# A different choice of seven-product tiles, and a different order in the first tiles, of four gated feed-forwards

## The reference, cut to what matters

```python
def rms_norm(x, w):
    xf = x.astype(jnp.float32)
    y = xf * lax.rsqrt(jnp.mean(xf * xf, axis=-1, keepdims=True) + EPS)
    return (y * w.astype(jnp.float32)).astype(x.dtype)

def swiglu(h, w_gate, w_up, w_down):
    return (jax.nn.silu(h @ w_gate) * (h @ w_up)) @ w_down

    for i in range(DEPTH):
        x = x + 0.5 * swiglu(rms_norm(x, ffn1_norm[i]), ffn1_w_gate[i], ffn1_w_up[i], ffn1_w_down[i])
        x = x + hybrid_mixer(...)
        x = x + 0.5 * swiglu(rms_norm(x, ffn2_norm[i]), ffn2_w_gate[i], ffn2_w_up[i], ffn2_w_down[i])
```

## Time and profile before

| | us |
|---|---|
| median of three runs | 2572.62 (2571.46 to 2574.76) |
| the profiled execution | 2572.15 |
| its span | 2570.4 |
| TensorE busy (matmuls) | 2488.7, 97% |
| VectorE, ScalarE, GpSimd busy | 1424.2, 1182.5, 1231.6 |
| mean granted TensorE clock | 0.991 of full speed |
| w_hi of a unit on ScalarE, mean | 1.01 |
| w_lo of a unit on GpSimd, mean | 2.36 |
| t_lo on GpSimd, one of two, mean | 2.60 |
| a unit's load, issue to landing, median | 3.5 |

### The profile page before, as it was taken

How to read it: one execution, slowest core, us unless ns; L and a number is a source line. 1 busy time by engine, 2 the same in 40 slices (tenths; PEclk the granted TensorE clock), 3 DMA queues, 4 the chain that set the end, 5 groups by cost and what they waited for, 6 DMA issues and landing times.

```text
span 2570.4 us, 34829 instructions
## 1 busy us (share of the span) xinstructions
PE 2488.7 (97%) x14086; PEld 2080.9 (81%) x14086; DVE 1424.2 (55%) x2049; ACT 1182.5 (46%) x1737; POOL 1231.6 (48%) x610
## 2 busy tenths in 40 slices
PE   8999999999989999999999989999999998999999
PEld 6888888777778898777878778898877766898887
DVE  6344352878563443586766753453587466443345
ACT  5332243568443333567455542332555675332333
POOL 3654654222455555446544255555444124555544
PEclk9999999999999999999999999999999999999999
DMA  3322333111313323222110123333332112323323
GB/s 130 115 95 87 115 111 111 58 58 50 106 60 109 103 91 107 82 89 84 50 34 27 53 96 92 106 99 95 96 98 82 41 50 75 114 91 99 107 91 123
DMA packets 61774, 223.43 MB, mean 87 GB/s; under 512 B 6704, under 2 KB 6832, under 8 KB 61488
## 3 DMA queue, kind: packets, MB, share of 16 engines
q1 hardware_dynamic: 60928, 218.07, 27.2%
q10 hardware_dynamic: 688, 3.15, 0.3%
HBM read 219.10 MB, written 2.10 MB: 86 GB/s over the span
## 4 chain that ended last, share of the span: by engine, by line
PE 75%; DVE 13%; ACT 6%; issue 3%; POOL 2%; DMA 1%; SPq 0%; DVEq 0%; ACTq 0%
PE ps L426 6%; PE ps L425 6%; PE ps L424 6%; PE ps L582 5%; PE ps L583 5%; PE ps L584 5%; PE ps L531 3%; PE ps L532 3%; PE ps L533 3%; PE ps L523 2%; PE ps L522 2%; PE ps L521 2%; PE ps L887 2%; PE ps L888 2%; PE ps L889 2%
## 5 line engine op out<-in xcount | busy, mean ns | idle before, releaser
L2859 POOL TENSOR_TENSOR w_lo<-raw,w_hi 128x1024 fp32r<-128x1024 f32 (+1 forms) x405 | 952.5, 2359 | 1199.0 <-ACT w_hi L445 1198.6
L445 ACT ACTIVATE w_hi<-raw 128x1024 fp32r<-128x1024 f32 (+1 forms) x405 | 409.6, 1012 | 479.6 <-PE ps L426 282.1
L582 PE MATMUL ps<-x_hi,w_hi 128*128 128x512 f32 x784 | 309.3, 395 | 13.1 <-DVE x_lo L483 7.4
L583 PE MATMUL ps<-x_lo,w_hi 128*128 128x512 f32 x784 | 306.5, 391 | 0.0
L584 PE MATMUL ps<-x_hi,w_lo 128*128 128x512 f32 x784 | 306.1, 390 | 0.0
L424 PE MATMUL ps<-mid_hi,w_hi 128*128 128x512 f32 x736 | 286.3, 389 | 0.0
L425 PE MATMUL ps<-mid_lo,w_hi 128*128 128x512 f32 x736 | 286.3, 389 | 0.0
L426 PE MATMUL ps<-mid_hi,w_lo 128*128 128x512 f32 x736 | 286.3, 389 | 0.0
L793 DVE SCALAR_TENSOR_TENSOR h<-ps,h 128x512 f32<-128x512 f32 x128 | 87.5, 691 | 266.8 <-PE ps L426 266.8
L636 ACT ACTIVATE ff_gate<-ff_gate 128x512 f32<-128x512 f32 x88 | 55.4, 630 | 372.3 <-DVE ff_gate L752 321.2
L2866 POOL TENSOR_TENSOR t_lo<-t_sum,t_hi 128x1024 fp32r<-128x1024 f32 x78 | 201.2, 2601 | 8.9 <-ACT t_hi L450 8.9
(11 more groups left out here) (449 smaller groups left out, 5780.0 us busy)
## 6 DMA issues: line engine op xcount, KB each, us to landing
raw<-in_units_dram SPq DMA_DIRECT2D x406, 512.0 KB, 3.5
...
```

What stands on the lines that cost most here:

```text
L445: nc.scalar.activation(w_hi[:, n % W_SLOTS, begin:], raw[:, n % RAW_SLOTS, begin:], ACT.Copy).then_inc(s_whi, 1)
L582: nc.tensor.matmul(out, hi, x_hi[:, k, :], start=(k == 0), stop=False)
L583: nc.tensor.matmul(out, hi, x_lo[:, k, :], start=False, stop=False)
L2859: nc.gpsimd.tensor_tensor(w_lo[:, n % W_SLOTS, begin:], raw[:, n % RAW_SLOTS, begin:], w_hi[:, n % W_SLOTS, begin:].bitcast(F32), ALU.subt ...
```

## The change

- **STRASSEN.** In chunks 1 and 2 of every feed-forward the seven-product tiles are 0, 1, 3, 5 instead of 0, 2, 4; in chunk 3 (four tiles) 0, 1, 3 instead of 0, 2. In chunk 0 of FF2 to FF4 they are 3 and 5 instead of 2 and 4; chunk 0 of FF1 keeps tile 4. The total is 51 instead of 39, and 37 plain tiles are left of 49.
- **Banks and buffers by parity.** A seven-product tile uses the banks and the ff_gate and ff_up halves of its own parity (pair = t % 2), as plain tiles do; the lent bank is 2 + pair of the other group. x_part lies elsewhere in SBUF.
- **The sequence of two neighbours.** If tile t + 1 is by seven products too, strassen_first(t + 1) is called inside strassen_rest(t), ahead of mid_lo of t. The weight sums of a chunk's tile 1 are made after side 1's additions to h of the chunk before.
- **Chunk 0.** ScalarE does rstd before the w_hi of units 3 and 4 (FF2 to FF4), or after them and before x_part (FF1), and each sx_hi comes behind a tile's mid_hi; VectorE makes both sx_lo after the tile two before the first seven-product one. FF1's activation sums are made behind its tiles 0 and 1. TensorE waits for the sums ahead of the second product of the first such tile, not ahead of the first.

```diff
-STRASSEN = (((4,), (0, 2, 4), (0, 2, 4), (0, 2)),) + (((2, 4), (0, 2, 4), (0, 2, 4), (0, 2)),) * 3
+STRASSEN = (((4,), (0, 1, 3, 5), (0, 1, 3, 5), (0, 1, 3)),) + (((3, 5), (0, 1, 3, 5), (0, 1, 3, 5), (0, 1, 3)),) * 3
...
-        x_part = place("x_part", M, [P, 8, HT])
+        x_part = place("x_part", M + 24 * KB, [P, 8, HT])
...
-            a, b, c = ps[:, 4 * g, 0:HT], ps[:, 4 * g + 1, 0:HT], ps[:, 4 * (g ^ 1) + 3, 0:HT]
+            a, b, c = ps[:, 4 * g + 2 * pair, 0:HT], ps[:, 4 * g + 2 * pair + 1, 0:HT], ps[:, 4 * (g ^ 1) + 2 + pair, 0:HT]
...
             pe.wait_ge(s_free, need + 1)
+            if first:
+                pe.wait_ge(s_xsum, 15 * w.ffn + 15)
             sum_product(b, 1, summed(1), True)
...
-            act_x_parts(act, w, own)
+            if not late:
+                act_x_parts(act, w, own)
...
                 if half == 0:
-                    ahead = 3
-                    act_ahead(act, n0, 0, 0)
-                    act_x_sums(act, w)
-                    act_ahead(act, n0, 0, 1)
+                    ahead = 2
                     if late:
-                        act_ahead(act, n0, 0, 2)
+                        act_ahead(act, n0, 0, 0)
+                        act_ahead(act, n0, 0, 1)
                         act_rstd(act, w, 4 * (g ^ 1), eps)
+                        act_x_parts(act, w, own)
                     else:
                         act_rstd(act, w, 4 * (g ^ 1), eps)
-                        act_ahead(act, n0, 0, 2)
+                        act_ahead(act, n0, 0, 0)
+                        act_ahead(act, n0, 0, 1)
...
                     nc.scalar.activation(mid_hi[:, t, :], product, ACT.Copy).then_inc(s_mhi, 1)
+                    if half == 0 and picked[0] - 3 <= t < picked[0] - 1:
+                        act_x_sum(act, w, t - picked[0] + 3)
...
-                    nc.vector.tensor_tensor(up, up, ff_gate[:, 0, :], ALU.mult).then_inc(s_prod, 1)
+                    nc.vector.tensor_tensor(up, up, ff_gate[:, pair, :], ALU.mult).then_inc(s_prod, 1)
+                    if t + 1 in picked:
+                        strassen_first(t + 1)
                     dve.wait_ge(s_mhi, mids + t + 1)
...
                     if t in picked:
-                        strassen_first(t)
+                        if t - 1 not in picked:
+                            strassen_first(t)
...
+                        if half == 0 and late and t < 2:
+                            dve_x_sums(dve, w, own, t)
+                        if half == 0 and t == picked[0] - 2:
+                            dve_x_sums_lo(dve, w, 0)
+                            dve_x_sums_lo(dve, w, 1)
...
                     dve_add_to_h(dve, w, tiles // 2, side, scale, gain, half == 3)
-                    if side == 0 and half < 3:
-                        dve_weight_sums(dve, S_OF[n0 + 3 * tiles])
+                    if half < 3 and side in STRASSEN[w.ffn][half + 1]:
+                        dve_weight_sums(dve, S_OF[n0 + 3 * tiles + 2 * side])
```

More of the change, by code:

```diff
@@ new lines, in dve_x_sums_lo, with dve_ffn @@
+        def dve_x_sums_lo(dve, w, i):
+            dve.wait_ge(s_xpart, 10 * w.ffn + 8 + i + 1)
+            nc.vector.tensor_tensor(sx_lo[:, 2 * i:2 * i + 2, :, :].rearrange("p a b t -> p (a b t)"),
+                                    sx_sum[:, 2 * i:2 * i + 2, :, :].rearrange("p a b t -> p (a b t)"),
+                                    sx_hi[i][:, :, :, :].rearrange("p a b t -> p (a b t)").bitcast(F32), ALU.subtract).then_inc(s_xsum, 1)
+        def dve_ffn(dve, w, scale, own, gain, split_p=False, late=False):
+            if not late:
+                dve_x_sums(dve, w, own, 0)
+                dve_x_sums(dve, w, own, 1)
@@ L714, in plain @@
                         dve_weight_sums(dve, S_OF[n0 + 2 * picked[0]])
-                    if half == 0 and t == 0:
-                        dve_x_sums_lo(dve, w)
                     dve.wait_ge(s_used, n0 + u + 2)
@@ L751, in strassen_rest @@
                     dve.wait_ge(s_sv, 7 * x + 5)
-                    nc.vector.tensor_tensor(ff_gate[:, 0, :], gate, rstd[:, :], ALU.mult).then_inc(s_free, 1)
+                    nc.vector.tensor_tensor(ff_gate[:, pair, :], gate, rstd[:, :], ALU.mult).then_inc(s_free, 1)
                     dve.wait_ge(s_used, n + 2)
```

65 lines of the change are left out of this document (29 added, 36 removed).

## The result

The kernel after takes 2657.59 us (median of four runs, 2652.22 to 2661.06) against 2572.43 (2571.46 to 2574.76) for the kernel before on the same chip: ratio 1.0324, 95% interval 1.0312 to 1.0336. The medians differ by 85.2 us.

The account below looks back on a forecast made before the run. The prediction took the kernel to be as long as TensorE's matmul stream and its gaps (busy 2488.7 of 2570.4 us). Seven terms summed to +73.7 on 2572.15, giving 2645.9 us, range 2608 to 2676.

Parts of the forecast that it names:

- forecast case: Whole kernel: stall at chunk ends, stall at heads, clock falling at most ends; 2645.9 us, chance 0.55.
- d: Tile 5 in 8 chunks of six tiles: TensorE waits some 0.6 us for t_lo; +4.8 us, bounds 0 and 12.
- f: Chunk 0 of FF1: the 5.70 us gap goes, but t_lo for tile 4 comes late; +4.5 us, bounds -8 and +8.
- g: Behind the chunk-end stops: TensorE's clock falls to half at most of 15, 1.5 us each; +22.5 us, bounds 0 and 51.
- a: Three more seven-product tiles in each feed-forward, 12 in all, each 0.84 us shorter than plain; -10.1 us.
- b: End of 15 chunks, ahead of the squares: TensorE waits 3.65 us for the last tile's second eviction; +54.8 us.
- c: Head of 12 chunks: GpSimd's turn between VectorE's weight-sum subtractions makes TensorE wait 1.3 us; +15.6 us.
- e: Chunk 0 of FF2 to FF4: lost time falls from 13.8 to 7.7 us each; -18.4 us, bounds -40 and 0.
- Full clock: Rival at chunk ends: the stops come but the clock does not fall; 2623 us, chance 0.20.
- long falls: Rival at chunk ends: each gap brings 6.8 us at half rate, 3.4 lost; 2674 us, chance 0.13.
- The end wait is met in time: Rival at chunk ends: banks_free is already there, so no stop or clock fall; 2568.5 us, chance 0.06.
- First tiles give back all: Rival in chunk 0 of FF2 to FF4: no gap left, -40 us there; 2624 us, chance 0.06 shared with another case.

Follow-up runs that it names:

- x_end: The kernel after, with TensorE starting the last squares in the three free banks and waiting only ahead of the lent fourth bank: 2578.19 us, ratio 1.0015.
- x_head: The kernel after, with VectorE's weight sums of tile 1 moved behind tile 0's copy and add: 2641.52 us, ratio 1.0267.
- x_d: The kernel after, with ScalarE's w_hi copy for the unit four further on taken ahead of a seven-product tile's own Silu: 2658.03 us, ratio 1.0328.
- x_ff1: The kernel after, with FF1's first chunk alone back in the old order: 2655.2 us, ratio 1.0316.
- x_c0: The kernel after, with chunk 0 of FF2 to FF4 reordered: both sx_hi right behind the norm, sx_lo behind tile 0's evictions: 2658.38 us, ratio 1.0323.
- x_dummy: The kernel after, end wait kept, with 15 unread matmuls of 512 columns ahead of it: 2633.51 us, ratio 1.0233.

## Why the prediction was right, point by point

It gave 2646 us, range 2608 to 2676, and slower with a chance of 0.94; 2657.6 came. The forecast case held (end stall, head stall, the clock falls), and the sum was 73.7 where 88.9 were measured between the profiled executions and 85.2 between the medians. What is missing lies in d, f and g, all three too small. Differences of whole chunks give the terms:

| term | predicted | measured | |
|---|---|---|---|
| a, 12 more seven-product tiles | -10.1 | -10.1 | rates as before |
| b, 15 stops at the end | +54.8 | +54.8 | 14 of 3.63, one of 3.98 |
| c, 12 heads | +15.6 | +14.6 | 1.22 each |
| d, tile 5's weights | +4.8 | +11.9 | the rest of chunks 1 to 3, net of 2.5 lost there before |
| e, chunk 0 of FF2 to FF4 | -18.4 | -18.4 | -6.4, -6.1, -5.9 without their ends |
| f, chunk 0 of FF1 | +4.5 | +7.8 | 87.84 against 80.03 for its tiles |
| g, the clock behind the stops | +22.5 | +28.0 | 1.87 on average |
| sum | +73.7 | +88.6 | |

- **b** was right in place, cause and size. The chain that had run beside a plain tile is 3.75 us from the last matmul's start. x_end shows that it is a matter of one bank: three were free all the time.
- **c** was right: GpSimd got one turn inside the four subtractions. The Trainium skill (SBUF - State Buffer, section "SBUF: two separate sides") has the lock held for one instruction; 1.78 us for the one subtraction beside GpSimd's half unit and 0.68 or 0.69 for the others agree. x_head gave back 14.7.
- **g** was mis-sized, by counting on ends without a fall and by taking the price from the middle. In the profiled execution all 15 stops were followed by half clock, thirteen at 1.6 to 1.8 us and two at 2.7 and 3.0, where the half clock lasted 6.8 us. The window 9 to 20 of the earlier trace rows, where single gaps of 1.7 us left the clock at 1.00, was no guide for 3.6. In x_head and x_d it was 15 of 15 again, in x_ff1 14 and in x_c0 13, so it is not quite certain each time. The Trainium skill (TensorE: Matmul & The Clock Gate, section "HAM oscillation - how this bites in real kernels") says that a wait in a loop, if it is long enough, puts the array back to half rate each time round; the 15 falls here agree, and the 14 and 13 of the two other executions are short of "each time".
- **d** was the term most off, and came out at its upper bound of 12; 9.4 us of it are at tile 5. The 11.6 us from the unit's arrival to t_lo held: from the start of the sums to that of t_lo it is 889.19 to 898.17, 8.98 us, and in the earlier trace rows 9.00. The step that was off is the one ahead of it, the moment at which unit 11's slot comes free. The prediction had GpSimd split unit 9 by T0 + 40.0, at 2.4 us a unit. Units 8 and 9 took 2.85 each, beside VectorE's product and mid_lo, and the split ended at 885.54, T0 + 41.1. So unit 11 landed at T0 + 44.7 instead of 43.7, and TensorE went on at T0 + 56.2 instead of 55.3. It asked at T0 + 55.2 instead of 54.7, since tile 3 had lost some 0.4 already. That makes 1.0 us in this chunk and 0.9 to 2.0 in the eight, where 0.6 was forecast. The losses at tile 3, up to 0.65 us, had been put at nothing.
- **e** had its wait right even in time: TensorE was to stand from 740.5 to 745.4; moved by FF2's later start (734.78 against 705.49) the trace has 740.6 to 744.7. The line for sx_lo is gone as said, and one for t_lo took its place. That the term came out to the tenth is luck. The forecast lost 4.9 us in this wait, 1.5 at tile 5 and 1.3 in small gaps. In FF2 the wait cost 4.2 us, the half clock behind it 2.7, tile 5 nothing and the small gaps some 0.5; in FF3 and FF4 the wait cost 5.0 and 5.2 and the half clock 2.3 and 2.8. Half clock behind this wait stood in no term of the sum, and what was put too high elsewhere made up for it.
- **f** had the chain right and its end 2.5 us early (t_lo at 72.3, in the trace at 74.8). Of the w_lo waits it named those of 1.8 and 1.7 us, and from start to start they cost 1.8 and 2.3; one of 1.7 between them it did not see. The clock fell during the long wait, not only behind it, so that tile 4's products began at half rate; this cost 2.5 us.
- **The rivals.** Full clock is excluded by the 15 falls, long falls by x_dummy's 23 us (51 was its price). "The end wait is met in time" is excluded by the 15 rows. "First tiles give back all" did not happen either, and the later runs show why: a wait taken away there comes back on the next engine.
